# Where the activations lie in SBUF: rows of 1024 or 1280 bytes at a fixed distance from the weights

## The reference

```python
def first_block(...):
    for layer in range(2):
        u = rms_norm(h, g_mix[layer])
        h = h + (mla_stick_breaking_mixer(u, ...) if layer == 0 else chunk_band_mixer(u, ...))
        u = rms_norm(h, g_ffn[layer])
        h = h + (silu(u @ w_gate[layer]) * (u @ w_up[layer])) @ w_down[layer]
    return rms_norm(h, g_final)

def second_block(x, ...):
    stream = concatenate([meta, x])                      # 272 tokens
    proj = rms_norm(stream, g) @ w_in                    # conv, q, k, v, index and gate columns
    y_a = conformer_conv_branch(u_conv, ...)             # depthwise conv of 31 taps, layer norm, silu, @ pw_out
    y_b = dsa_sparse_attention(q, k, v, q_idx, k_idx, w_idx, w_o)    # each query sees its top 68 keys
    stream = stream + (g_a * y_a + g_b * y_b) @ w_merge_out
    up = causal_depthwise_conv(rms_norm(stream, g2) @ ffn_up, ...)   # 3 taps
    a, b = split(up)
    stream = stream + (silu(a) * b) @ ffn_down
    return rms_norm(stream, g3)[16:]
```

## Time and profile before

| | |
|---|---|
| three runs | 1147.68, 1148.07, 1149.96 us; median 1148.07 |
| the profiled execution | 1148.63 us, its span 1146.8 us |
| TensorE | busy 1098.3 us (96%), mean granted clock 0.981 |
| VectorE, ScalarE, GpSimd | busy 751.3, 576.0, 214.8 us |
| DMA | 181.36 MB, mean 158 GB/s |

### The profile page before, as it was taken

How to read it: one execution, slowest core, us unless ns; L and a number is a source line. 1 busy time by engine, 2 the same in 40 slices (tenths; PEclk the granted TensorE clock), 3 DMA queues, 4 the chain that set the end, 5 groups by cost and what they waited for, 6 DMA issues and landing times.

```text
span 1146.8 us, 22301 instructions
## 1 busy us (share of the span) xinstructions
PE 1098.3 (96%) x8813; PEld 1071.1 (93%) x8813; DVE 751.3 (66%) x1232; ACT 576.0 (50%) x840; POOL 214.8 (19%) x198
## 2 busy tenths in 40 slices
PE   7998999999999999999999899988999889999998
PEld 7996999999999999999999799987999889999997
DVE  6766565555667776565555457998775657788753
ACT  5666554443554555444454434434656446655542
POOL 1432030001131111100000167773440000000000
PEclk9999999999999999999999899997999999999999
DMA  8734256656775343565456344451335443555460
GB/s 262 213 121 136 65 178 189 202 162 198 237 225 172 119 145 99 187 195 184 146 178 207 111 147 148 147 161 61 111 110 185 143 151 126 168 183 172 139 203 37
DMA packets 187925, 181.36 MB, mean 158 GB/s; under 512 B 17935, under 2 KB 186268, under 8 KB 187851
## 3 DMA queue, kind: packets, MB, share of 16 engines
q1 hardware_dynamic: 187323, 178.23, 49.1%
q0 software_dynamic: 528, 2.10, 0.6%
HBM read 179.27 MB, written 1.05 MB: 157 GB/s over the span
## 4 chain that ended last, share of the span: by engine, by line
PE 82%; DVE 8%; ACT 5%; POOL 3%; issue 2%; DMA 0%; SPq 0%; ACTq 0%; POOLq 0%; DVEq 0%
PE ps L547 25%; PE ps L548 24%; PE ps L549 24%; DVE ps L2488 2%; ACT w_hi L370 2%; POOL work L473 2%; POOL w_lo L398 1%; PE ps L2014 1%; PE ps L2039 1%; PE ps L456 1%; PE ps L2040 1%; PE ps L1896 1%; DVE gates L2550 1%; PE ps L1903 0%; DVE top L2546 0%
## 5 line engine op out<-in xcount | busy, mean ns | idle before, releaser
L547 PE MATMUL ps<-u_hi,w_hi 128*128 128x256 f32 (+2 forms) x1800 | 518.0, 288 | 14.3 <-DVE u_lo L516 6.9
L548 PE MATMUL ps<-u_lo,w_hi 128*128 128x256 f32 (+2 forms) x1800 | 511.6, 284 | 0.0
L549 PE MATMUL ps<-u_hi,w_lo 128*128 128x256 f32 (+2 forms) x1800 | 510.7, 284 | 0.0
L386 DVE TENSOR_TENSOR w_lo<-raw,w_hi 128x2048 fp32r<-128x2048 f32 (+3 forms) x157 | 326.5, 2090 | 147.4 <-ACT w_hi L370 147.0
L547 PEld LDWEIGHTS ps<-u_hi,w_hi 128*128 128x128 f32 x1800 | 343.8, 191 | 17.2 <-issue 13.0
L548 PEld LDWEIGHTS ps<-u_lo,w_hi 128*128 128x128 f32 x1800 | 343.5, 191 | 0.7
L549 PEld LDWEIGHTS ps<-u_hi,w_lo 128*128 128x128 f32 x1800 | 344.1, 191 | 0.0
L370 ACT ACTIVATE w_hi<-raw 128x2048 fp32r<-128x2048 f32 (+3 forms) x182 | 316.4, 1753 | 39.4 <-PE ps L549 29.1
L547 PE MATMUL ps<-a_hi,w_hi 128*128 128x256 f32 x528 | 146.0, 276 | 0.0
L548 PE MATMUL ps<-a_lo,w_hi 128*128 128x256 f32 x528 | 145.9, 276 | 0.0
L549 PE MATMUL ps<-a_hi,w_lo 128*128 128x256 f32 x528 | 145.8, 276 | 0.0
(11 more groups left out here) (327 smaller groups left out, 1321.8 us busy)
## 6 DMA issues: line engine op xcount, KB each, us to landing
raw<-in_w_in SPq DMA_DIRECT2D x24, 1024.0 KB, 5.4
raw<-in_w_gate SPq DMA_DIRECT2D x22, 1024.0 KB, 5.3
raw<-in_w_up SPq DMA_DIRECT2D x22, 1024.0 KB, 5.4
raw<-in_ffn_up SPq DMA_DIRECT2D x22, 1024.0 KB, 5.1
raw<-in_w_down SPq DMA_DIRECT2D x16, 768.0 KB, 4.4
raw<-in_od_w_qkv SPq DMA_DIRECT2D x12, 1024.0 KB, 5.3
raw<-in_w_down SPq DMA_DIRECT2D x16, 640.0 KB, 4.4
raw<-in_ev_w_in SPq DMA_DIRECT2D x7, 1024.0 KB, 10.4
```

Source lines behind the costliest of these rows:

```text
L386: nc.vector.tensor_tensor(w_lo[t % RING][:, 0:n], raw[t % RAW][:, 0:n], w_hi[t % RING][:, 0:n].bitcast(F32), ALU.subtract).then_inc(lo_don ...
L547: nc.tensor.matmul(out_ap, a_h, b_h, start=start and n == 0, stop=False)
L548: nc.tensor.matmul(out_ap, a_h, b_l, start=False, stop=False)
L549: mm = nc.tensor.matmul(out_ap, a_l, b_h, start=False, stop=stop and n == len(pairs) - 1)
```

## The change

It moves tensors in SBUF. `u` becomes two sets on the same space: `u_hi`, `u_lo` with rows of 256 columns (1024 bytes) for the first block, and `m_hi`, `m_lo` with rows of 320 columns (1280 bytes), of which 258 or 272 are used, for the second. A filling of 48 columns (192 bytes) ahead of them puts both at 192; 1024 and 1280 are multiples of 256, so every kt lies there. `work` now starts at 192 as well (its rows stay at 1088 bytes). Fillings of 16 and 32 columns keep `a` and `lat` at 192 and bring `o`, `o3`, `q_b`, `k_b`, `k_cat`, `v_s` and `v_odd` there. `o2_hi` stays at 64, `o2_lo` goes from 160 to 128, both with rows of 1032 bytes. What is read from column 14 or 16 of `m` starts 56 or 64 bytes behind 192, at 248 or 0.

The space for it comes from small tensors that are laid on others: `x_root` and `q_pad` on what `u` leaves free in the first block, the last two heads of the bias too, `cva` and `cvb` on `work`, `ki` on `rstd`, `first_cols` on `log_ms`.

```diff
+U_PITCH, U_SHIFT = 320, 48
+SHIFT = 16
...
     h = sb("h", [P, KT, T2])
-    u_hi = sb("u_hi", [P, KT, T2], F32R)
-    u_lo = sb("u_lo", [P, KT, T2], F32R)
+    sb("u_place", [P, U_SHIFT])
+    with ExitStack() as t:
+        u_hi = sb("u_hi", [P, KT, T1], F32R, scope=t)
+        hi_rest = sb("hi_rest", [P, KT * (U_PITCH - T1)], scope=t)
+        u_lo = sb("u_lo", [P, KT, T1], F32R, scope=t)
+        lo_rest = sb("lo_rest", [P, KT * (U_PITCH - T1)], scope=t)
+    m_hi = sb("m_hi", [P, KT, U_PITCH], F32R)
+    m_lo = sb("m_lo", [P, KT, U_PITCH], F32R)
+    x_root, q_pad = hi_rest[:, 0:T1], lo_rest[:].rearrange("p (e n) -> p e n", e=2)
...
-    x_root = sb("x_root", [P, T1])
+    sb("scope_place", [P, SHIFT])
...
+        sb("o_place", [P, 2 * SHIFT], scope=s)
...
-        q_pad = sb("q_pad", [P, 2, T1], scope=s)
...
-        cva = sb("cva", [P, 2, 2, T1], scope=s)
-        cvb = sb("cvb", [P, 2, 2, T1], scope=s)
...
+        sb("o3_place", [P, 2 * SHIFT], scope=s)
...
-        bias_h = sb("bias_h", [P, C_H, 2 * P], scope=s)
+        bias_h = sb("bias_h", [P, C_H - 2, 2 * P], scope=s)
...
+    cva, cvb = (flat_work[:, n * 4 * T1:(n + 1) * 4 * T1].rearrange("p (s t n) -> p s t n", s=2, t=2) for n in range(2))
...
+    biases = [bias_h[:], lo_rest[:].rearrange("p (h n) -> p h n", h=2)]
+    ki = rstd
+    first_cols = log_ms[:, 0:KT * CONV_W].rearrange("p (k w) -> p k w", w=CONV_W)
...
     def u_h(n):
-        return lambda kt: u_hi[:, kt, 0:n]
+        return lambda kt: (u_hi if n == T1 else m_hi)[:, kt, 0:n]
...
-        nc.gpsimd.dma_start(bias_h[:], rel).then_inc(sem("bias_landed"), 16)
-        pool.wait_ge(sem("bias_landed"), 16)
-        own = bias_h[:, :, 0:P]
-        nc.gpsimd.tensor_tensor(own, own, c("chunk_mask")[:, ::-1].unsqueeze(1).to_broadcast([P, C_H, P]), ALU.add)\
-            .then_inc(sem("bias_masked"), 1)
-        pool.wait_ge(sem("bias_masked"), 1)
+        for at, t in ((0, biases[0]), (C_H - 2, biases[1])):
+            rel = bass.AP(tensor=od_rel_bias.tensor, offset=od_rel_bias.offset + 513 * at + 1 + P,
+                          ap=[[1, P], [513, t.shape[1]], [1, 2 * P]])
+            nc.gpsimd.dma_start(t, rel).then_inc(sem("bias_landed"), 16)
+        pool.wait_ge(sem("bias_landed"), 32)
+        for n, t in enumerate(biases):
+            own = t[:, :, 0:P]
+            nc.gpsimd.tensor_tensor(own, own, c("chunk_mask")[:, ::-1].unsqueeze(1).to_broadcast([P, t.shape[1], P]), ALU.add)\
+                .then_inc(sem("bias_masked"), 1)
+            pool.wait_ge(sem("bias_masked"), n + 1)
...
-                               [(hi[:, kt, at], lo[:, kt, at], u_hi[:, kt, cols], u_lo[:, kt, cols])], kt == 0, kt == KT - 1)
+                               [(hi[:, kt, at], lo[:, kt, at], m_hi[:, kt, cols], m_lo[:, kt, cols])], kt == 0, kt == KT - 1)
```

24 lines of the change are left out of this document (10 added, 14 removed).

## The result

The changed kernel took 1144.2 us (median of 8 runs, 1138.98 to 1146.18), the kernel before 1149.88 (8 runs, 1147.68 to 1151.5): a ratio of 0.9949, 95% interval 0.9931 to 0.9968. It is faster by 5.7 us where 20.6 were forecast. The profiled executions are 1144.12 and 1148.63 us.

A forecast was written before the change was run, and what follows sets the result against it. The pace of one `product` matmul on TensorE was taken as the bound. Terms 9.4 + 6.1 + 0.3 + 1.8 + 2.4 + 0.7 = 20.7 us took 1148.6 to 1127.9, adjusted to 1127.5 us; range 1121 to 1142.

The forecast's parts named there:

- likeliest case: In the ffn loops, 256 and 258 columns both run in the short rhythm; chance 0.71, from 1120 to 1136.
- part 1: ffn0 and ffn1, 256 columns of `u`, all rows to 192: 4.9 ns a matmul, 9.4 us in all.
- entered at a hiccup: In ffn loops, a hiccup at TensorE's jump back every four units lets a stream enter the short rhythm, 113.3 ns.
- Part 2: ffn2, 258 columns of `m`: 114.2 ns against 120.0, 6.1 us; down2's slow start goes too, 0.3 us.
- Part 3: pw and merge, 384 matmuls of 258 columns: 5.8 ns each, less what lies in waits, 1.8 us.
- the start of down2: The slow start of down2, 72 matmuls, goes as well: 0.3 us.
- at any distance: In streams of `product`, the long rhythm, 118 ns, is stable whatever the distance; the short, 113.3, needs every row at 192.
- stages with attention: in, out0, qkv, out1: broken streams can fall into either rhythm; about half of 5.2 us taken, 2.4 us.
- Part 5: mix: 456 matmuls of 272 columns could save up to 2.7 us, VectorE bounds the middle; 0.7 us taken.
- the first rival: Streams stay in the long rhythm: 0.3 ns a matmul won in `u` of 256 columns, 1145.5 us; chance 0.10.
- The rival that 258 columns don't hold it: 258 columns don't hold the short rhythm while 256 do: about 1136 us; chance 0.10.
- the slower rival in mix: 672 matmuls of mix at 248 and 0 fall on the worst interval, +5.4 us, giving 1151; chance 0.05.

The follow-up runs named there:

- 260 columns: Changed kernel with the products of ffn2 over 260 columns in place of 258, the two more read by nobody: 1150.36 us, ratio 1.0014.
- wait: Changed kernel with TensorE waiting for its own last matmul of the norm before the third unit of ffn0 and ffn1: 1141.62 us, ratio 0.9925.
- wait and matmul: Changed kernel with that wait before the third unit of ffn0 and ffn1, then one matmul of 16 columns: 1147.63 us, ratio 0.9981.
- the two with float32 pairs: Changed kernel with two 16-column float32 matmuls ahead of unit 2 of ffn0, ffn1 and each down-loop turn: 1153.51 us; also 258-column rows at 64: 1149.52.
- 258 at 64: Changed kernel with the 258-column rows of `m` (pw, merge, ffn2) 64 bytes behind the weights instead of 192: 1141.51 us, ratio 0.9960.
- bare streams: Five kernels with only `product`'s three matmuls over eight kt and four tiles, stream after stream; not the reference's computation, compared only within themselves.
- before with the wait: Kernel before the change, with TensorE's wait before the third unit of ffn0 and ffn1: 1148.22 us, ratio 0.9985.
- one float32 matmul, 258 at 64: Changed kernel with 258-column rows at 64, plus one 16-column float32 matmul ahead of unit 3 of ffn0, ffn1 and down2's fifth unit: 1142.96 us, ratio 0.9958.

## Why the prediction was wrong

The likeliest case was put at 0.71 and didn't come. Of the 20.7 us in the sum 4.5 were measured between the two profiles, and two steps failed.

The first is in part 1: "entered at a hiccup", with "a hiccup every four units in each ffn loop" behind it. The hiccups at the loop's jump belonged to the mixed rows; with all rows at one distance the jump leaves no trace. A stream keeps what it started with through the whole stage and into the next, until other matmuls or a wait break it, and a break can as well bring the long rhythm: the same reading of the earlier trace rows, in which a stall freed down2, should have been read the other way too. In eight profiles with `u` at 192 (the changed kernel twice, 260 columns, wait, wait and matmul, the two with float32 pairs, 258 at 64) ffn0 ran short in five of eight and ffn1 in two of eight. What picks the rhythm behind a norm's wait stays open.

The second cost more. Parts 2 and 3 took it that 258 columns hold the short rhythm, "since the rhythm is kept by the rows' starts, which are alike". They don't: the pace was 118.7 to 122.2 ns at each of eight distances, 120.8 in ffn2. The two parts, without the start of down2, were put at 7.9 us and came to -2.6, of which some 1.7 are the clock.

What was right is that the distance sets the pace, that mixed rows take 118.2 and rows at 192 can take 113.3. Two readings beside it were not: the long rhythm isn't stable "at any distance" (at 0 there is only 120.0), and the short one isn't bound to 192 (it stands at 64 in bare streams; the 117.9 of out1 was the long one of two).

Term by term, in us won (the table of starts):

| term | forecast | measured |
|---|---|---|
| 1 ffn0, ffn1 | 9.4 | 4.5 + 0.3 |
| down1 | 0 | -2.4 |
| 2 ffn2, start of down2 | 6.4 | -1.0 |
| 3 pw, merge | 1.8 | -1.6 |
| 4 stages with attention | 2.4 | 1.0 + 0.8 |
| 5 mix, with wo | 0.7 | 2.9 |
| sum | 20.7 | 4.5 |

- *Part 1.* ffn0 gave what was forecast, 4.5 of 4.7. ffn1 won only the difference of the long rhythm to the mixed rows, as the first rival had it, priced there at 0.3 ns a matmul.
- *down1* is in no term. It lay at 192 before as well, and I took its short rhythm as its own. But a down stage takes over the rhythm of the stage ahead. Behind the mixed rows down1 came out short in both profiles (before, and before with the wait); now ffn1 hands its long rhythm on, and 528 matmuls by 4.5 ns are 2.4 us. It is the largest thing that none of the rivals has.
- *Part 2*, where 5.8 ns by 1040 matmuls are 6.0 us and not 6.1, had no such rhythm to win. At 192 258 columns are at 120.0 or 120.8, and ffn2, 119.8 in much of the kernel before, went to 120.8: 1.0 us lost. The rival that 258 columns don't hold it was right, at 0.10; by itself it would have given 1136. The fast start of down2 came, 7.5 us for 67 instead of 64 matmuls, and went into the wait behind it: the stage is as long as before.
- *Part 3.* No pace was won, and the stretch had a lower granted clock than before, 0.97 for 1.00 over some 56 us, which is 1.7 us; the second profile of the changed kernel has 0.97 there too. These are the windows of pw and merge, before and after, TensorE alone:

```profile
891.90:947.10 55.20, 48.61 (x393) 1.00 0.47 153
```

```profile
884.80:941.60 56.80, 50.23 (x393) 0.97 0.45 149
```

- *Part 5* was mis-sized, though the middle of mix, where VectorE was said to be the bound, gave only 0.5 us (35.3 us from 722.2 to 757.6 before, 34.8 after). The tiles of 272 columns went from 126.8 to 123.3 ns (9.0 us for 71 and for 73 matmuls, of before and of after below), 1.6 us on 456. The rest of the 2.9 us isn't the pace: the granted clock over mix and its tail was 0.95 before and 0.96 after. The clearest piece is mix's start, whose first 120 matmuls took 17.8 us before, with a granted clock of 0.50 in the first 4.3 us, and 14.9 after, with 1.00 there; half of that is lost again further on. These are half-clock stretches that moved, for which the prediction allowed 2 us.

```profile
723.00:732.00 9.00, 9.00 (x73) 1.00 0.37 117
```

```profile
717.00:726.00 9.00, 9.00 (x75) 1.00 0.38 116
```

- The bias, the small tensors laid elsewhere and the slower rival in mix cost nothing that shows.

The forecast of the sign held, and the range missed by 2 us. It was cut off at half of the long-rhythm case, and the case that came, one pair short and one long with 258 columns slow, was between two rivals that were each priced as if the other did not occur together with it.

How far the executions of one kernel lie apart can be read off the profiled ones, whose rhythms are known:

| kernel | ffn0 and down0, ffn1 and down1 | that execution, us |
|---|---|---|
| one float32 matmul, 258 at 64 | short, short | 1135.2 |
| wait and matmul | short, short | 1139.3 |
| changed | short, long | 1144.1 |
| changed, again | short, long | 1143.2 |
| 258 at 64 | long, short | 1140.8 |
| 260 columns | long, long | 1148.4 |

A pair of stages is worth 108.9 to 113.1 and 59.7 to 62.1, so 6.6 us together, and two pairs 13, which is near the spread of 14 us of the kernel with the wait. That the spread comes from this is likely and not shown, since each kernel has one profile, or two. All short, the changed kernel would be near 1137.5 (an estimate: 1144.1 less the 6.6 of ffn1 and down1), which is still 10 above the forecast: the other terms were wrong by themselves.

What stays open is what the moment of release and the matmul between set in TensorE, and so what decides behind a wait in the kernel. In a running stream the same boundary does the same each time: one float32 matmul of 16 or 128 columns and two of 256 turn the rhythm over in the kernel, while in the bare streams one of 16 or 128 turned long to short and then left it short. Why the two differ no run tells. No version here beats the changed kernel beyond its interval: the wait alone, at 0.9925 [0.9901, 0.9948], comes nearest, but its interval overlaps that of the changed kernel, and its profile has the same rhythms. That it is better isn't shown.

## What to carry to other kernels

When a stream of equal matmuls is the bound, don't put its moving rows at a multiple of 256 bytes from the weights, try one distance for all of them, and read the pace from starts, stage by stage. Here the choice is worth some 23 us between 0 and 192, but only 5.7 against rows at mixed distances, and 64 was 0.3% slower than these. Where a pace has two values in the trace of one shape, ask what each stage starts with and what it hands to the next, before counting the better value for all; a gain that hangs on such an entry is a distribution, and its price is the share of entries that come out right. And look at equal stages that already have the good value: they can lose it.

## What was not expected of the hardware

- At distances 64 and 192 a stream of 256 columns has two exact rhythms, 113.3 and 117.8 ns, at 0 only 120.0, elsewhere 116.6 to 120.0. Two columns more (258) cost 6.7 to 7.6 ns at 192 and have 118.7 to 122.2 over all distances; 272 columns are at 123.3 to 123.5 at 160 and 192 and 125 to 127 elsewhere.
- A rhythm holds for over a thousand matmuls, through hardware loops and from stage to stage, at a granted clock of 1.00 in both. Two float32 matmuls of 256 columns in the running stream turned it over each time, eight added ones and eleven of the kernel's own, and one of 16 or 128 columns six times of six; a release 15 ns later did so in the bare streams.
- The Trainium skill, "TensorE: Matmul & The Clock Gate", section "Back-to-back issue gap", gives N / 2.4 + 2.5 ns for a matmul by itself, an estimate of 109.2 ns for 256 columns, and says that in a stream the weight loads set the spacing as well; the prediction held the rule against a stream. No stream here, bare or not, came below 113.3. By "SBUF — State Buffer", section "Who interferes with whom", the two read ports are independent; that the pace hangs on where moving and stationary rows lie to one another, with nothing else running, speaks against that for this pair of reads.
